# The state-space stage of a hybrid decoder step: 46 projection blocks as three rounded products each, with the rests subtracted on VectorE, the first convolution tap on ScalarE, and the group norm at a later place

## The chip, the cores and the metric

The program runs on one core of one Trainium2 chip. The metric is the device time of one execution in microseconds (us). The core has TensorE (PE: matrix products; its weight loads are PEld), VectorE (DVE), ScalarE (ACT), GpSimd (POOL) and SyncE (SP, which here only issues transfers). Each engine takes its own instructions strictly in order and waits on semaphores for the others.

## The reference, cut to what matters

One inference step of a decoder layer for 512 prompt tokens and 8 x 4 sample tokens (544 columns in all), with three branches (latent attention, state space, memory attention), a gated merge and a feed-forward part. Before the branches stands one projection of the 1024-wide input. The change lies in the state-space branch:

```
xbc = silu(conv_b + sum(conv_w[k] * xbc_ext[:, k:k + L] for k in range(4)))     # 24 chunks of 128 channels
per chunk of 128 tokens:
    y = (C.B * decay * dt) @ x + C @ S * exp(cum);   S = S * exp(last) + (wb * B).T @ x
y = (y + d_skip * x) * silu(z)
yg = y per group of 512 channels (4 groups);  yg *= rsqrt(mean(yg * yg) + eps);  y = yg * ssm_norm_g
```

All numbers are float32, and the matrix products have to come out near that precision.

## The kernel before, in words

Everything is kept transposed: channels on the 128 partitions, the 544 tokens on columns. The weights come as a stream of blocks of 128 x 1024 floats (512 KB) into a ring of four slots (`RING`); one block gives 128 output channels over all 544 tokens, written as two halves of 272 columns to one of two PSUM accumulators, `acc0` and `acc1`, in turn. `project` (L1721, matmuls at L1731) multiplies a block: 2 halves x 8 chunks = 16 float32 matmuls. SyncE's `load` (L552) fetches a block when the block three before it has begun (`blocks_begun`).

The state-space stage is block 0 (dt, 32 channels, L1841), blocks 1 to 6 (the six convolution chunks of group 0) and ten blocks for each of the four groups. The later stages (`out`, `up`, `down`) already use the other way: ScalarE rounds a block to the format fp32r (L701), GpSimd subtracts the rounded part from the block (L522), and `products` (L1771) multiplies in three passes of fp32r: high x high, high x low, low x high, 48 matmuls a block.

In this text the ten blocks of a group g are called b1 to b10. b1 to b4 are the four z chunks of group g; b5 to b10 are the convolution chunks 0 to 5 of group g+1 (in the last group: five latent chunks and the rotary one). Between them TensorE does the group's own products: it turns x and B (`turn`, before and inside b2, after b2), multiplies B by C (inside b3), adds up chunk states (before b4), reads out the four head pairs (`read_out` 0 to 3: before b5, before b6, before b8, before b9), and does the sample states (`sample_y` before b7, `state_adds` inside b7, before b8, inside b8, inside b9).

ScalarE empties an accumulator for a convolution chunk (`evac`, L715 to L718), or reads a z chunk (`z_read`, L775, L776), computes the decays (`decays`, L789 to L793) and the tanh of the gates (L724). VectorE does the convolution (`conv`, L1198: the left edge L1200, two small saves L1202 and L1203, the first tap L1208, three more taps L1214), closes the gate (`finish`, L1222 and L1224), weighs the decays (L1316), reads out y (L1369), gates it (L1374), adds the sample states (`add_state`, L1379), and norms the group before: a reciprocal (`group_reciprocal`, L1271) and four products (`group_norm`, L1276). GpSimd scales C (L470) and the sample states (L476) and adds squares (L482 to L488). The order of each engine's queue is written out by hand in these functions; nothing reorders it.

## Time and profile before

| | us |
|---|---|
| median of 3 executions | 1715.8 (1713.83 to 1717.81) |
| the profiled execution | 1717.8 |
| its span in the profile | 1716.1 |
| PE busy | 1667.9 (97%) |
| DVE busy | 758.8 (44%) |
| ACT busy | 408.4 (24%) |
| POOL busy | 405.9 (24%) |

Busy is the sum of an engine's instructions, over the whole span. The engines' shares differ much from stage to stage: the stage of this change takes the first 456 us. Times in the trace are counted from the start of the span. A matmul in float32 is recorded as two instructions (x32 is one block of 16), one in fp32r as one; the duration of the whole run of them is what counts.

### The profile page before, as it was taken

The page shows a single profiled execution, that of the slowest core. Times are in us where ns is not written, and L with a number is a line of the kernel's source. Part 1 is how long each engine was busy: PE and PEld are TensorE (multiplying, and loading weights), DVE is VectorE, ACT ScalarE, POOL GpSimd, SP SyncE. Part 2 cuts the span into 40 slices and gives each one's busy share as a digit, 9 for nine tenths or more (in the row PEclk, how much of TensorE's full clock was granted, in tenths as well). Part 3 has the DMA queues.
Part 4 walks back from the last instruction along what each step waited for, and adds up shares of the span by engine and source line. Part 5 has one row for each costly group of instructions (what it writes and reads, how often), then busy time and mean ns, then how long its engine had stood idle before and what let it go on. Part 6 is the DMA issues. An engine that isn't in the chain of part 4 may idle for free.

```text
span 1716.1 us, 25873 instructions
## 1 busy us (share of the span) xinstructions
PE 1667.9 (97%) x10438; PEld 1410.6 (82%) x10438; DVE 758.8 (44%) x1312; ACT 408.4 (24%) x800; POOL 405.9 (24%) x344
## 2 busy tenths in 40 slices
PE   8999999999999999999999999999996999999995
PEld 6878787787877777787777777779996999999995
DVE  5567687774431111112122122344378761177334
ACT  2252433425221211111111110142234111111122
POOL 0041231314020000000332300014345333344432
PEclk9999999999999999999999999999998999999998
DMA  5425133352362221223787764432321322222211
GB/s 193 148 80 175 66 124 123 94 179 80 114 212 71 62 74 62 62 77 117 229 254 235 236 241 181 151 123 87 99 86 39 89 93 89 86 87 87 87 62 53
DMA packets 70411, 206.24 MB, mean 120 GB/s; under 512 B 10162, under 2 KB 26803, under 8 KB 65683
## 3 DMA queue, kind: packets, MB, share of 16 engines
q1 hardware_dynamic: 50384, 151.67, 27.5%
q10 hardware_dynamic: 13762, 31.93, 5.3%
q0 software_dynamic: 6144, 20.98, 4.0%
q8 instruction: 83, 1.36, 0.3%
q14 instruction: 38, 0.30, 0.1%
HBM read 189.68 MB, written 14.86 MB: 119 GB/s over the span
## 4 chain that ended last, share of the span: by engine, by line
PE 87%; DVE 8%; issue 1%; ACT 1%; DMA 1%; POOLq 0%; POOL 0%; SPq 0%; DVEq 0%; ACTq 0%
PE acc L1731 29%; PE acc L1771 29%; PE acc L2069 7%; PE acc L2036 3%; PE acc L2019 2%; PE acc L2172 1%; PE bank L2084 1%; PE bank L2103 1%; PE bank L2085 1%; PE bank L2124 1%; DVE work L1214 1%; PE bank L2186 1%; PE bank L2054 1%; PE bank L2060 1%; PE bank L2257 1%
## 5 line engine op out<-in xcount | busy, mean ns | idle before, releaser
L1731 PE MATMUL acc<-xt,ring 128*128 128x272 f32 x2272 | 542.7, 395 | 0.0
L1731 PEld LDWEIGHTS acc<-xt,ring 128*128 128x128 f32 x2272 | 425.9, 190 | 99.5 <-issue 15.7
L1771 PE MATMUL acc<-x_parts,f_parts 128*128 128x272 f32 x1408 | 220.5, 293 | 12.4 <-DVE x_parts L1141 11.4
L522 POOL TENSOR_TENSOR f_parts<-ring,f_parts 128x1024 fp32r<-128x1024 f32 x65 | 157.6, 2425 | 247.9 <-ACT f_parts L701 247.7
L1771 PEld LDWEIGHTS acc<-x_parts,f_parts 128*128 128x128 f32 x1408 | 197.6, 192 | 14.4 <-issue 8.0
L500 POOL DMA_DIRECT2D work<-in_page_cols x128 | 68.8, 538 | 464.2 <-PE bank L2124 354.3
L1771 PE MATMUL acc<-f_parts 128*128 128x272 f32 x1344 | 172.3, 289 | 0.0
L1771 PEld LDWEIGHTS acc<-f_parts 128*128 128x128 f32 x1344 | 170.4, 188 | 0.1
L701 ACT ACTIVATE f_parts<-ring 128x1024 fp32r<-128x1024 f32 x65 | 69.0, 1061 | 238.4 <-PE acc L1771 204.2
L2069 PE MATMUL acc<-branch,ring 128*128 128x272 f32 x512 | 120.0, 392 | 0.0
L2069 PEld LDWEIGHTS acc<-branch,ring 128*128 128x128 f32 x512 | 96.0, 190 | 18.8
L1694 DVE TENSOR_SCALAR f_parts<-attended 128x544 fp32r<-128x544 f32 x32 | 76.2, 2382 | 1.1
L1214 DVE SCALAR_TENSOR_TENSOR work<-work,vecs 128x600 f32<-128x600 f32 x72 | 68.4, 950 | 2.4
L1771 PE MATMUL acc<-f_parts,mg_parts 128*128 128x272 f32 x528 | 68.8, 289 | 0.0
L1771 PEld LDWEIGHTS acc<-f_parts,mg_parts 128*128 128x128 f32 x528 | 67.3, 188 | 0.2
L522 POOL TENSOR_TENSOR mg_parts<-ring,mg_parts 128x1024 fp32r<-128x1024 f32 x21 | 50.5, 2403 | 71.4 <-ACT mg_parts L701 71.4
L1731 PE MATMUL acc<-attended,ring 128*128 128x272 f32 x256 | 63.1, 406 | 0.5 <-DVE attended L1603 0.5
L1771 PE MATMUL acc<-x_parts,mg_parts 128*128 128x272 f32 x480 | 62.1, 289 | 0.5 <-DVE attended L1688 0.5
L1771 PEld LDWEIGHTS acc<-x_parts,mg_parts 128*128 128x128 f32 x480 | 61.0, 188 | 0.7 <-DVE attended L1688 0.7
L1731 PEld LDWEIGHTS acc<-attended,ring 128*128 128x128 f32 x256 | 50.0, 197 | 12.3 <-issue 1.2
L1678 DVE TENSOR_TENSOR xt<-xt,acc 128x544 f32<-128x544 f32 x11 | 7.9, 721 | 111.8 <-PE acc L1771 111.8
L470 POOL TENSOR_TENSOR work<-work 128x384 f32<-128x384 f32 x32 | 37.1, 1158 | 75.2 <-ACT work L793 75.2
(351 smaller groups left out, 2046.3 us busy)
## 6 DMA issues: line engine op xcount, KB each, us to landing
ring<-in_stream SPq DMA_DIRECT2D x216, 512.0 KB, 3.6
work<-in_page_cols POOLq DMA_DIRECT2D x128, 160.0 KB, 3.3
attended<-in_ssm_state ACTq DMA_DIRECT2D x8, 1024.0 KB, 6.3
work<-cum_rows SPq DMA_DIRECT2D x32, 256.0 KB, 4.5
out_ssm_s<-attended ACTq DMA_DIRECT2D x8, 1024.0 KB, 5.5
work<-in_ckv_rows ACTq DMA_DIRECT2D x64, 128.0 KB, 3.5
work<-in_ckv_rows SPq DMA_DIRECT2D x64, 128.0 KB, 3.1
work<-in_memk_cols SPq DMA_DIRECT2D x8, 1024.0 KB, 6.7
```

The lines of the kernel that those rows point to most:

```text
L470: pool.tensor_tensor(r, r, C_[:, P:SEQ], MUL).then_inc(sem["c_scaled"], 1)
L500: pool.dma_start(keys[kq][:, i * KEYS_W:(i + 1) * KEYS_W], page_cols[p]).then_inc(sem[f"keys_in_slot{kq}"], 16)
L522: pool.tensor_tensor(lo, ring[:, s * BLOCK:(s + 1) * BLOCK], hi.bitcast(F), SUB).then_inc(sem["split_ready"], 1)
L701: act.activation(hi, ring[:, s * BLOCK:(s + 1) * BLOCK], ACT.Copy).then_inc(sem["hi_ready"], 1)
L1214: dve.scalar_tensor_tensor(out=c, in0=ext[j][:, i:i + CL], scalar=tap(i), in1=c, op0=MUL, op1=ADD).then_inc(sem[signal], 1)
L1694: dve.tensor_scalar(hi, q, 1.0, None, MUL).then_inc(sem["dve_step"], 1)
L1731: m = pe.matmul(acc[p][:, half, 0:width], w[:, k * P:(k + 1) * P], x(kk)[:, half * width:(half + 1) * width], start=kk == 0, stop=kk == n_ ...
L1771: m = pe.matmul(acc_half, w[:, k * P:(k + 1) * P], x[:, kk, of], start=kk == 0 and n == 0, stop=kk == last and n == 2)
L2019: m = pe.matmul(acc[p][:, 0, 0:N_MEM], w[:, k * P:(k + 1) * P], mem[:, k, :], start=k == 0, stop=k == KC - 1)
L2036: m = pe.matmul(acc[p][:, half, 0:HT], w[:, c * 256 + off:c * 256 + off + P], cq[:, c, half * HT:(half + 1) * HT], start=c == 0, stop=c == 2)
L2054: m = pe.matmul(bank[0][:, :], w[:, c * P:(c + 1) * P], ckv[:, c, 0:SEQ], start=c == 0, stop=c == 1)
L2069: m = pe.matmul(acc[1][:, half, 0:HT], w[:, k * P:(k + 1) * P], BR[:, kk, half * HT:(half + 1) * HT], start=kk == 0, stop=kk == 2 * KC - 1)
```

## The change

For blocks 1 to 46 (`SSM_SPLIT`) `project` gives way to `project_x` with three fp32r products, as in the later stages. The input x is split once at the start: ScalarE rounds its 8 chunks into XL, VectorE turns XL into the rest, and ScalarE then writes the rounded part over x itself (`xt_hi` lies where `xt` lay), chunk by chunk as the dt block has read it. Each weight block is rounded by ScalarE into one of two buffers (`high_part`), and VectorE writes the rest back over the ring slot (`low_part`). The rounding of a block waits until the block before it has begun. x is loaded again at the first block after the stage, and the memory tokens are loaded at the end of the stage instead of early. ScalarE now does the left edge and the first tap of each convolution chunk, right behind its evacuation, and VectorE starts a chunk on `tap_ready`. The halving of some constants goes to the start of VectorE's queue. The reciprocal and the four products of the group norm go from the first part of a group to between b6 and b9.

```
+            def high_part():                              # ScalarE
+                at = hi_at.next()
+                if at > SSM_SPLIT:
+                    return
+                s = at % RING
+                act.wait_ge(sem["blocks_begun"], CREDIT["blocks_begun"] + at)
+                act.wait_ge(sem[f"weights_in_slot{s}"], 16 * (loaded_before(at, s) + 1))
+                act.activation(w_hi[at % 2], ring[:, s * BLOCK:(s + 1) * BLOCK], ACT.Copy).then_inc(sem["hi_ready"], 1)
...
             def evac(j):
+                high_part()
+                n = evacuated.next()
+                ch = n - 1
+                if n > 2:
+                    act.wait_ge(sem["conv_ready"], n - 2)
+                act.activation(ext_s(j)[:, :, 0:3], st_conv[:, ch, :, :], ACT.Copy)
                 act.wait_ge(sem[f"acc{j}_ready"], t.next(f"acc{j}_ready"))
                 act.activation(v2(ext[j][:, 3:3 + T]), accv(j), ACT.Copy)
...
+                act.wait_ge(sem[f"acc{j}_free"], t.next(f"acc{j}_free"))
+                act.activation(cacc[j][:, 0:CL], ext[j][:, 0:CL], ACT.Identity, scale=tap,
+                        bias=V("convb", ch)).then_inc(sem["tap_ready"], 1)
...
                 def z_read(hp):
                     j, a = hp % 2, (hp + 1) % 2
+                    high_part()
...
+            def low_part():                               # VectorE
+                at = lo_at.next()
+                if at > SSM_SPLIT:
+                    return
+                slot = slice(at % RING * BLOCK, (at % RING + 1) * BLOCK)
+                dve.wait_ge(sem["hi_ready"], t.next("hi_ready"))
+                dve.tensor_tensor(ring_lo[:, slot], ring[:, slot], w_hi[at % 2].bitcast(F),
+                        SUB).then_inc(sem["split_ready"], 1)
...
             def conv(g, q, between=None):
                 j, ch = (q + 1) % 2, g * QC + q
-                dve.tensor_scalar(ext_s(j)[:, :, 0:3], st_conv[:, ch, :, :], 1.0, None, MUL)
-                dve.wait_ge(sem[f"acc{j}_free"], t.next(f"acc{j}_free"))
+                low_part()
+                dve.wait_ge(sem["tap_ready"], t.next("tap_ready"))
...
-                dve.tensor_scalar(c, ext[j][:, 0:CL], tap(0), V("convb", ch), MUL, ADD).then_inc(sem["dve_step"], 1)
...
+            low_part()
             conv(0, 0)
...
+                low_part()
                 z_gate(0)
                 turned(2, 3)
-                if g:
-                    group_reciprocal()
                 turned_samples()
-                if g:
-                    group_norm(g - 1)
+                low_part()
...
                 weigh(5)
+                if g:
+                    group_reciprocal()
                 read_y(1)
...
                 ahead_finish(1)
+                if g:
+                    group_norm(g - 1, (0, 1))
                 add_state(2)
...
+            def project_x(p, between=None):               # TensorE
+                at = used.value()
+                next_block()
+                wh, wl = w_hi[at % 2], ring_lo[:, at % RING * BLOCK:(at % RING + 1) * BLOCK]
+                pe.wait_ge(sem[f"acc{p}_free"], t.next(f"acc{p}_free"))
+                pe.wait_ge(sem["split_ready"], t.next("split_ready"))
+                for half, of in enumerate(halves):
+                    if half and between:
+                        between()
+                    for k in range(KC):
+                        if at == 1 and half == 0:
+                            pe.wait_ge(sem["x_split"], t.next("x_split"))
+                        first, m = products(acc[p][:, half, 0:HT], wh, wl, XH, XL, k, k, KC - 1, of)
...
+            sp.wait_ge(sem["y_ready"], GC * GROUPS)
+            sp.dma_start(mem, mem_t).then_inc(sem["mem_loaded"], 16)
+            load(3)
+            sp.wait_ge(sem["blocks_begun"], CREDIT["blocks_begun"] + SSM_SPLIT + 2)
+            sp.dma_start(X, x_t).then_inc(sem["x0_loaded"], 16)
```

`low_part` is called ten times in a group: for b3 ahead of `z_gate(0)`, for b4 behind the turned samples, for b5 in the middle of the state sums, for b6 ahead of `z_gate(3)`, and then at the head of each of the six `conv`, for b7 to b10 and the next group's b1 and b2. ScalarE's `high_part` for a block stands at the head of the evacuation of the block two before it.

The first place is the head of VectorE's queue, from its first instruction on. Before, it holds the dt computation alone (32 rows) and then the convolution:

```order
L1148 TENSOR_SCALAR work<-acc,vecs 32x544
L1152 SCALAR_TENSOR_TENSOR work<-work 32x544
L1156 TENSOR_SCALAR work<-work 32x544
L1158 TENSOR_SCALAR work<-work 32x544
L1161 TENSOR_SCALAR work<-work 32x544
```

Now (L1126 is the rest of x, L1121 the rest of a weight block):

```order
L1126 TENSOR_TENSOR ssm_parts<-xt,ssm_parts 128x544 x8
L1121 TENSOR_TENSOR ring_lo<-ring,ssm_parts 128x1024
L1135 TENSOR_SCALAR vecs<-vecs 128x24
L1135 TENSOR_SCALAR vecs<-vecs 128x120
L1138 MEMSET work 128x3 x2
L1248 TENSOR_SCALAR work<-acc,vecs 32x544
```

The rest of block 1 is made ahead of the dt computation, that of block 2 behind all of it.

The second place is VectorE's queue in groups 1 and 2 around b8, from the first two sample states to the third and fourth. Before (L1379 the sample states, L1200 to L1214 one convolution chunk, L1222 and L1224 the gate of the one before):

```order
L1379 TENSOR_TENSOR attended<-attended,bank 128x512 x2
L1200 TENSOR_SCALAR work<-work 128x8x3
L1202 TENSOR_SCALAR work<-work 128x3
L1203 TENSOR_SCALAR work<-work 128x24
L1208 TENSOR_SCALAR work<-work,vecs 128x600
L1214 SCALAR_TENSOR_TENSOR work<-work,vecs 128x600 x3
L1222 SCALAR_TENSOR_TENSOR branch<-work 128x512
L1224 SCALAR_TENSOR_TENSOR branch<-work 128x32
L1379 TENSOR_TENSOR attended<-attended,bank 128x512 x2
```

Now (the sample states are L1469, the chunk L1293 to L1302, the gate L1310 and L1312, two products of the group norm L1365):

```order
L1469 TENSOR_TENSOR attended<-attended,bank 128x512 x2
L1121 TENSOR_TENSOR ring_lo<-ring,ssm_parts 128x1024
L1293 TENSOR_SCALAR work<-work 128x3
L1294 TENSOR_SCALAR work<-work 128x24
L1302 SCALAR_TENSOR_TENSOR work<-work,vecs 128x600 x3
L1310 SCALAR_TENSOR_TENSOR branch<-work 128x512
L1312 SCALAR_TENSOR_TENSOR branch<-work 128x32
L1365 SCALAR_TENSOR_TENSOR branch<-branch,vecs,work 128x544 x2
L1469 TENSOR_TENSOR attended<-attended,bank 128x512 x2
```

Between the two pairs of sample states a rest (L1121) and two norm products have come in; the left edge and the first tap have gone.

The third place is ScalarE's queue at the end of the same group, for the chunks of b7 and b8. Before (L717 and L718 empty an accumulator, L724 is a gate's tanh, L833 a square):

```order
L833 ACTIVATE work<-branch 128x544 x2
L717 ACTIVATE work<-acc 128x544
L718 ACTIVATE work<-acc 128x8x4
L724 ACTIVATE work<-work 128x600
L717 ACTIVATE work<-acc 128x544
L718 ACTIVATE work<-acc 128x8x4
```

Now (L710 is the rounding of the block after the next, L784 the left edge, L791 the first tap):

```order
L710 ACTIVATE ssm_parts<-ring 128x1024
L784 ACTIVATE work<-work 128x8x3
L786 ACTIVATE work<-acc 128x544
L787 ACTIVATE work<-acc 128x8x4
L791 ACTIVATE work<-work,vecs 128x600
L796 ACTIVATE work<-work 128x600
```

The evacuation now stands behind a rounding, which itself waits for the next block to begin.

## Rows read from the trace of the kernel before

**Rows 1.** Engines by stretch, one row per group: length, busy (instructions), PEclk, DMA share, GB/s
```profile
core 0: us, PE busy (x) PEld busy (x) DVE busy (x) ACT busy (x) POOL busy (x), PEclk, DMA share, GB/s
70.94:169.38 98.44, 97.80 (x553) 76.43 (x553) 67.45 (x115) 34.53 (x82) 25.66 (x21) 1.00 0.35 115
169.38:268.66 99.28, 97.89 (x553) 76.42 (x553) 73.57 (x120) 38.00 (x85) 25.62 (x21) 1.00 0.36 120
...
367.93:456.38 88.45, 87.25 (x499) 68.44 (x500) 42.87 (x62) 35.98 (x76) 24.04 (x20) 1.00 0.30 100
```

**Rows 2.** Chain that ended last: start, length, what (one float32 block; four product blocks)
```profile
192.76 7.33 PE acc L1731 x32
...
1252.54 24.14 PE acc L1771 x192
```

**Rows 3.** Timeline of group 1, starts of b7 and b8, and two decays on ScalarE
```profile
192.80 1.28 ACT L789 ACTIVATE work<-work 128x128 f32<-128x128 f32 x4 [2.88 <-PE bank L1925]
...
195.06 1.26 ACT L789 ACTIVATE work<-work 128x128 f32<-128x128 f32 x4
...
222.60 3.93 PE L1731 MATMUL acc<-xt,ring 128*128 128x272 f32 x16
...
232.85 3.83 PE L1731 MATMUL acc<-xt,ring 128*128 128x272 f32 x16
```

**Rows 4.** Chain that ended last, start of b9 in group 1
```profile
243.12 3.86 PE acc L1731 x16
```

**Rows 5.** Timeline of the first phase: dt on VectorE, blocks 1 to 3 on TensorE
```profile
14.82 22.27 PE L1731 MATMUL acc<-xt,ring 128*128 128x272 f32 x96
15.03 0.77 DVE L1148 TENSOR_SCALAR work<-acc,vecs 32x544 f32<-32x544 f32 x1 [15.03 <-PE acc L1841]
...
30.14 0.22 DVE L1185 COPY work<-work 32x128 f32<-32x128 f32 x1
```

**Rows 6.** VectorE by form, 138.48 to 237.77: busy, mean ns | idle before
```profile
L1208 DVE TENSOR_SCALAR work<-work,vecs 128x600 f32<-128x600 f32 x6 | 4.1, 688 | 0.2
...
L1271 DVE RECIPROCAL work<-work 128x544 f32<-128x544 f32 x1 | 3.5, 3541 | 0.0
L1276 DVE SCALAR_TENSOR_TENSOR branch<-branch,vecs,work 128x544 f32<-128x544 f32 x4 | 2.9, 781 | 0.0
...
L1288 DVE TENSOR_TENSOR work<-bank,work 128x512 f32<-128x512 f32 x4 | 2.7, 683 | 2.4 <-PE bank L1896 2.4
```

**Rows 7.** VectorE by form, 1100 to 1716: a subtraction of a rounded part
```profile
L1640 DVE TENSOR_TENSOR f_parts<-xt,f_parts 128x544 fp32r<-128x544 f32 x8 | 5.2, 717 | 0.3 <-ACT f_parts L985 0.3
```

**Rows 8.** ScalarE, the rounding of a block (costliest groups of the page)
```profile
L701 ACT ACTIVATE f_parts<-ring 128x1024 fp32r<-128x1024 f32 x65 | 69.0, 1061 | 238.4 <-PE acc L1771 204.2
```

**Rows 9.** ScalarE by form, 138.48 to 237.77: gate and evacuation
```profile
L724 ACT ACTIVATE work<-work 128x600 f32<-128x600 f32 x6 | 4.2, 701 | 17.9 <-DVE work L1214 17.9
...
L717 ACT ACTIVATE work<-acc 128x544 f32<-128x544 f32 x6 | 3.7, 621 | 17.2 <-PE acc L1731 17.2
```

**Rows 10.** Timeline of group 1: three taps with and without GpSimd beside them
```profile
197.48 1.10 POOL L470 TENSOR_TENSOR work<-work 128x384 f32<-128x384 f32 x1 [0.76 <-ACT work L793]
...
213.07 3.23 DVE L1214 SCALAR_TENSOR_TENSOR work<-work,vecs 128x600 f32<-128x600 f32 x3
...
214.43 1.23 POOL L470 TENSOR_TENSOR work<-work 128x384 f32<-128x384 f32 x1 [2.76 <-ACT work L793]
...
232.46 2.60 DVE L1214 SCALAR_TENSOR_TENSOR work<-work,vecs 128x600 f32<-128x600 f32 x3
```

**Rows 11.** Timeline: a longer pause of TensorE (in brackets)
```profile
990.79 1.08 PE L2120 MATMUL bank<-work 128*32 128x256 f32 x16 [2.06 <-DMA work<-in_page_cols]
```

**Rows 12.** Timeline: a shorter one
```profile
1019.50 3.73 PE L2186 MATMUL bank<-work,branch 128*128 128x256 f32 x16 [1.09 <-DVE mark L1598]
```

**Rows 13.** Stretches behind the two pauses (PEclk third from the end)
```profile
992.00:993.00 1.00, 1.00 (x9) 0.32 (x5) 0.00 (x0) 0.00 (x0) 0.00 (x0) 0.54 0.79 271
...
995.00:996.00 1.00, 1.00 (x7) 0.86 (x5) 0.68 (x2) 0.00 (x0) 0.00 (x0) 0.75 0.21 66
...
1021.00:1022.00 1.00, 1.00 (x7) 0.86 (x6) 0.37 (x2) 0.00 (x0) 0.00 (x0) 1.00 1.06 434
```

**Rows 14.** The stretch in which the memory keys are computed
```profile
463.00:470.00 7.00, 7.00 (x34) 6.11 (x33) 6.96 (x7) 1.26 (x3) 0.00 (x0) 1.00 0.50 150
```

More of the change, by code:

```diff
@@ L163 @@
               "o_m_ready", "mg_ready"]
-SEMAPHORES += [f"{n}_in_slot{i}" for n in ("keys", "rows") for i in range(4)]
+SEMAPHORES += [f"{n}_in_slot{i}" for n in ("keys",) for i in range(4)]
 SEMAPHORES += [f"x{c}_loaded" for c in range(KC // 2)]
@@ L263, in program @@
         k = Carver()
-        ext, cacc, th = ([k(EXT) for _ in range(2)] for _ in range(3))
+        XH, XL = chunks(xt_hi, KC), chunks(ssm_parts, KC)
+        w_hi = [ssm_parts[:, KC * T + j * BLOCK:KC * T + (j + 1) * BLOCK] for j in range(2)]
+        ext, cacc = ([k(EXT) for _ in range(2)] for _ in range(2))
+        th = [work[:, j * EXT + 3:(j + 1) * EXT + 3] for j in range(2)]
+        st_conv = k(NC * DEC_BATCH * 3).rearrange("p (c b t) -> p c b t", b=DEC_BATCH, t=3)
+        assert B_S_AT <= k.at
+        b_s = rounded_b[0:NS3, k.at - B_S_AT:k.at - B_S_AT + P]
+        k.at += P
+        dec_p = k(NB * SSM_HEADS).rearrange("p (c h) -> p c h", h=SSM_HEADS)
+        k.at = 6 * T
+        off_s = k(GW)
+        c_mask = k(DEC_BATCH * NS).rearrange("p (b t) -> p b t", t=NS)
+        ecum_s = k(SSM_HEADS)
+        k.at = 6 * EXT
         krope, a_rstd = k(T), k(T)
@@ L294, in program @@
         xw = k((NB + 1) * GW).rearrange("p (c n) -> p c n", n=GW)
-        xdt_at = k.at
+        xw_s = rounded[0:NS3, xw_at - ROUNDED_AT + NB * GW:xw_at - ROUNDED_AT + (NB + 1) * GW]
         xdt = k((NB + 1) * GW).rearrange("p (c n) -> p c n", n=GW)
-        xw_s = rounded[0:NS3, xw_at - ROUNDED_AT + NB * GW:xw_at - ROUNDED_AT + (NB + 1) * GW]
         xw_full = xdt[NS:2 * NS, NB, :]
-        mem = k(KC * N_MEM).rearrange("p (c m) -> p c m", m=N_MEM)
+        assert k.at <= parts_at
+        k.at = WORK - GC * SEQ
+        cum_r = [k(SEQ) for _ in range(4)]
+        mem_at = WORK - KC * N_MEM
+        mem = work[:, mem_at:WORK].rearrange("p (c m) -> p c m", m=N_MEM)
+        mv_at = 22282
+        mk_at = mv_at + 2 * 1024
+        assert mk_at + 8 * N_MEM <= mem_at
         decay = [xw[:, c, :] for c in range(NB)]
@@ L460, in _ @@
                 pool.wait_ge(sem["cb_read"], t.next("cb_read"))
+                pool.wait_ge(sem["add_ready"], t.next("add_ready", NB))
                 if g:
@@ L1036, in _ @@
             t = Counts(dve, {"acc0_free": 1, "acc1_free": 1})
+            lo_at = Count(None)
+            def low_part():
[6 more added lines that the diff above has]
+                        SUB).then_inc(sem["split_ready"], 1)
+            for c in range(KC):
+                dve.wait_ge(sem["rounded"], t.next("rounded"))
+                dve.tensor_tensor(XL[:, c, :], X[:, c, :], XL[:, c, :].bitcast(F), SUB).then_inc(sem["low_even"], 1)
+            t.skip("low_even", KC)
+            low_part()
             dve.wait_ge(sem["const_loaded"], 2 * 16)
@@ L1039, in _ @@
             dve.wait_ge(sem["acc0_free"], 1)
+            w0 = _V["convw"][0]
+            g0 = _V["bgate"][0]
+            for halved in (vecs[:, g0:g0 + 3 * KC], vecs[:, w0:w0 + NC * (CONV_W + 1)]):
+                dve.tensor_scalar(halved, halved, 0.5, None, MUL).then_inc(sem["dve_step"], 1)
+            dve.wait_ge(sem["dve_step"], t.next("dve_step", 2))
+            for j in range(2):
+                dve.memset(ext[j][:, 0:3], 0.0).then_inc(sem["dve_step"], 1)
+            dve.wait_ge(sem["dve_step"], t.next("dve_step", 2))
             def maxima(pairs, scale, signal):
@@ L1272, in group_reciprocal, with group_norm @@
                 dve.wait_ge(sem["dve_step"], t.next("dve_step"))
-            def group_norm(g):
-                for hp in range(GC):
+            def group_norm(g, hps=range(GC)):
+                for hp in hps:
                     dve.scalar_tensor_tensor(out=BR[:, g * GC + hp, :], in0=BR[:, g * GC + hp, :],
@@ L2151, in cached_values @@
                     pe.wait_ge(sem["s_new_turned"], t.next("s_new_turned"))
-                    for kq in range(4):
-                        pe.wait_ge(sem[f"rows_in_slot{kq}"], t.next(f"rows_in_slot{kq}", 4 * 16))
+                    pe.wait_ge(sem["rows_loaded"], t.next("rows_loaded", 16 * 16))
                     for i in range(4):
```

152 lines of the change are left out of this document (91 added, 61 removed).

## The prediction

> **What bounds the kernel now.** I first read the engines by stretch, cut at the starts of b2 [rows 1]. In groups 0 to 2 TensorE is busy for 97.8 of about 99 us and VectorE for 67 to 74; the last group takes 88.45. So TensorE's work sets the time, and VectorE is second with some 26 us to spare a group. The chain that ended last says the same [rows 2]: one float32 block runs 7.33 us from first to last matmul, unbroken. It also has the price of the new way: four product blocks take 24.14 us, 6.04 each. Ten blocks a group are 73 of TensorE's 99 us, the other 26 are the group's own products.
>
> Next to read is how tight the queues beside TensorE are, since the change puts ten roundings into ScalarE's queue, ten rests into VectorE's, and each product block must wait for both. For that I take single durations from the groups by form [rows 6 to 9] and lay one group out, engine by engine, in queue order.
>
> **Prices.** A product block saves 7.33 - 6.04 = 1.29 us of TensorE; 46 blocks, 59 us. A rounding is 1.06 us [rows 8]. A rest is not in the trace at this size: the same subtraction with 544 columns takes 0.72 [rows 7], 512 columns of another take 0.68 [rows 6], so 1.06 ns a column and 1.23 us for 1024, 1.15 when the next follows at once. I take 1.2; the ends are 0.95 (a float32 tensor-scalar form of the first tap, 0.69 for 600 columns [rows 6], scaled by columns, 1.17 at most) and 1.8 beside GpSimd (below). The first tap costs VectorE 0.6 to 0.7 today and the left edge 0.2; on ScalarE the tap is like its gate, 0.70 for the same 600 columns [rows 9]. So VectorE gains 10 x 1.2 and loses 6 x 0.8: 73.6 becomes 81 us a group, under TensorE's 86. By sums alone a group would be 86.5 us. It is the order that spoils it.
>
> **The start.** The dt block ends at 14.8 and VectorE then works on dt until 30.36; TensorE meanwhile runs blocks 1 to 3 without a gap, until 37.1 [rows 5]. Splitting x hides under the loads and the dt block (8 roundings and 8 rests of 0.7 us, done at about 12; the last rounded chunk 0.7 us after the dt block, and TensorE begins with the first). But the rest of block 2 stands behind the whole dt computation. Block 1 ends at 21, block 2 can begin at 30.4 + 1.2 = 31.6: TensorE idles 10.6 us. Then each block waits for the rest made behind the convolution of the chunk three before it. Counting through I get starts of blocks 2 to 7 at 31.6, 37.7, 45.1, 52.1, 58.2, 64.2, the sixth chunk done at 71.4, and b2 of group 0 at 73.2 instead of 70.9: 2.3 us lost.
>
> **One group (1 or 2), from the start of b2 as zero.** Starts before, from [rows 2 to 4], less 169.38, and after, as laid out:
>
> b4: 23.4, now 19.5. b7: 53.2, now 47.6. b8: 63.5, now 60.5. b9: 73.7, now 74.6. Next b2: 99.3, now 99.3.
>
> To b7 the group runs 5.6 us ahead: five faster blocks bring 6.4, reciprocal and norm (3.5 and 2.9 [rows 6]) are out of VectorE's way in b3, and about 2.3 go lost before b5. There the decays wait behind the rounding for b5, which waits for b4 to begin at 19.5: rounding, z3 and the sample decays until 22.1, two decays of 2.26 (start to start [rows 3]), and 1.1 for GpSimd's product [rows 10], so the read-out starts at 27.9 and not at 25.6.
>
> Then it is lost again, in three places.
> - *Inside b7.* `state_adds(0)` needs `read_y_s`, and VectorE gets to that so: weights 4 and 5 until 46.6, the reciprocal until 50.1, read-out 0.7, rest 1.2, one tap 0.9, `read_y_s` 0.7: 53.7. b7's first half is done at 50.6. TensorE waits 3.1.
> - *Inside b8.* VectorE ends sample states 0 and 1 at 60.1, and b8 can begin at 60.5. Only then does ScalarE round for b9 (61.65), and only behind that evacuate b7 (0.7) and do the tap (0.7): `tap_ready` at 63.15, though b7 was finished at 57.3. VectorE stands idle for 2 us, then saves, three taps 2.8, gate 0.83, two norm products 1.43, two sample states 1.2: 69.5. b8's first half is done at 63.5, TensorE waits 6 us. Before, the same stretch of VectorE's queue went on without a wait.
> - *At the end.* b9 begins at 74.6, so b10's rounding is ready at 75.8 and VectorE idled 3.6 us; the last chunk is gated at 97.4, while TensorE is through with b1 and the sums at 94.1: a wait of 3.3.
>
> These waits cost 12 us or so of the 12.8 that ten blocks save. The whole is even: 99.3.
>
> Two costs come on top. *GpSimd.* Three taps took 2.60 us alone and 3.23 with a GpSimd operation of 1.23 among them [rows 10]: half of the shared time is lost. On VectorE's tight stretch from 46 to 97 some 11 us of GpSimd work lie; about a quarter of it hits VectorE where it is late: 1.5 a group (0.5 in the last). *The clock.* After a pause of 2.06 us TensorE was granted 0.54, the 1.2 GHz level, from 992 on, though busy, and half of the slice from 995 still (0.75); after a pause of 1.09 it stayed at 1.00 [rows 11 to 13]. That is some 3.3 us at half speed, so I price a pause like this or longer at 3.3 / 2 = 1.65 beside itself, where TensorE is on the path behind it. That is so for two of the pauses in each of groups 0 to 2 (in b8, and at the end; the one in b7 has a spare us behind it), for one in group 3, and for the one at the start. Bounds: 0, and 3 for each.
>
> **Group 0** has no reciprocal and no norm: 95.8 laid out instead of 98.44. **Group 3** has no convolution ahead, so TensorE leads from b5 on: 81.2 instead of 88.45.
>
> **Behind the stage** x comes again, 2.2 MB, ahead of the block for the fourth memory key. The stretch moves 150 GB/s [rows 14] and 434 have been seen [rows 13], so both land 7 to 9 us after the issue, and the block is wanted 10.4 us (three of 3.47) after it: nothing, at most 2. The memory tokens come 1 MB, some 12 us before they are used: nothing.
>
> **Sum.** Start +2.3 and 1.65; group 0 -2.6 + 1.5 + 3.3; groups 1 and 2 twice 0 + 1.5 + 3.3; group 3 -7.2 + 0.5 + 1.65. Together +10.7. Against the profiled execution, 1717.8, that is 1728.5; this execution was 2.0 above the median of 1715.8, so I expect 1726.5. Its own range, with 2 us either way a group and the bounds of the clock: 1716 to 1742.
>
> **A rule against the trace.** The trace shows half of the shared time lost [rows 10]. The Trainium skill (SBUF — State Buffer, Who interferes with whom) says that a VectorE instruction with two SBUF inputs and a GpSimd instruction that reads SBUF exclude each other, and the second waits for the whole first. The rest is such an instruction and there are ten new ones a group; it would make the collisions dearer, the third rival below.
>
> **Rivals.**
> - *The waits are there, but they cost only themselves* (no clock loss, no collisions on the tight stretch). For: the shorter pause left the clock alone, and ten of GpSimd's operations fall in VectorE's own waits. Against: the pauses laid out are 3 to 6 us. Time: 1715.8 + 2.3 - 2.6 + 0 - 7.2 = 1708. It is the case on the other side; it decides as soon as the two extra costs stay under 7.5 us in all.
> - *TensorE stays the bound.* If ScalarE and VectorE keep up everywhere, 59 us less the 10.6 of the start: 1667. Against it: the evacuation of b7 and b8 cannot precede the next block's start, whatever the speeds.
> - *Collisions whole.* If each of the nine GpSimd operations on the tight stretch costs VectorE its whole 1.1 us and not a fraction, a group loses 10 and not 1.5: three times 8 more, 1750.
> - *In between:* half of the extra costs of 18.2 us, 1717.
>
> **How the numbers follow.** Forecast 0.53, waits alone 0.22, TensorE bound 0.05, whole collisions 0.08, in between 0.12. Below 0.2% (3.4 us) a measurement of this kernel can't be told from no change. Faster takes the second and third case and a little of the last: 0.29; same most of the last and the low edge of the forecast: 0.10; slower 0.61. The range that leaves out the bound case and the far ends of the others is 1702 to 1744.
>
> **What would show it.** TensorE idle from about 21 to 31.6, and b2 of group 0 at 73 to 76. Starts of b2 99 to 106 us apart in groups 1 and 2. In b7, b8 and at the group's end, TensorE waiting for VectorE, the longest (5 to 6 us) for the sample states in b8, and PEclk near 0.5 behind them. Rests of 1.2 us, up to 1.8 beside GpSimd. VectorE waiting for the first tap and for roundings. Wrong it is if b8 begins long before VectorE's first two sample states are in, if the evacuations come right behind their blocks, or if the groups shrink under 97 us.

## The result, and the profile after

The changed kernel takes 1754.4 us (median of 4 runs, 1751.51 to 1756.54) against 1716.7 for the kernel before on the same chip: ratio 1.0221, interval 1.0205 to 1.0238. Slower was forecast, at 1726.5; the measured time lies 10 us above the end of the range, 1744. The profiled execution is the one of 1751.51 us, span 1749.8, against 1717.8 and 1716.1 before: 33.7 us to explain.

The page of the changed kernel, its busy line, TensorE's granted clock in 40 slices, and the chain by engine:

```profile
PE 1635.0 (93%) x11174; PEld 1434.6 (82%) x11174; DVE 794.9 (45%) x1318; ACT 483.5 (28%) x910; POOL 404.1 (23%) x344
...
PEclk8998989989999999999999999999998999999998
...
PE 81%; DVE 9%; ACT 5%; issue 3%; DMA 1%; POOL 0%; POOLq 0%; ACTq 0%; SPq 0%; DVEq 0%
```

The first eleven slices of the clock are the changed stage. The stretches that answer to [rows 1], cut at the same places (groups 0 to 3 and the memory keys); columns as there:

```profile
76.97:184.55 107.58, 91.88 (x713) 83.02 (x713) 74.22 (x115) 49.76 (x104) 25.16 (x21) 0.92 0.31 101
184.55:293.93 109.38, 91.15 (x713) 82.24 (x713) 79.12 (x118) 53.21 (x107) 25.17 (x21) 0.92 0.34 109
293.93:406.43 112.50, 93.19 (x714) 84.07 (x713) 79.83 (x118) 53.21 (x107) 24.71 (x21) 0.91 0.33 109
406.43:492.95 86.52, 79.38 (x644) 71.91 (x644) 50.29 (x68) 44.50 (x86) 23.27 (x20) 0.96 0.34 113
492.95:528.15 35.20, 34.51 (x159) 29.41 (x158) 20.20 (x21) 5.64 (x13) 4.47 (x8) 1.00 0.67 226
```

TensorE was busy for 97.8 of 98 to 99 us of each group; now it is busy for 91 to 93 and stands for 16 to 19. The groups grew by 9.1, 10.1 and 13.2 us, the last one shrank by 1.9, and b2 of group 0 comes at 77.0 instead of 70.9, 6.0 later. The sum is 36.6; the memory keys take 0.5 more than before, and the code behind them, which the change leaves alone, 3.3 less in this execution (its granted clock is 0.99 there and was 0.98). What TensorE waited for, from 15 to 500 us (total, times, longest):

```profile
PE bank L2099 <- DVE attended L1469: 17.0, 4, 5.6
PE bank L2099 <- DVE branch L1488: 16.2, 4, 4.7
PE bank L2014 <- DVE work L1312: 14.5, 4, 4.7
PE acc L1869 <- DVE ring_lo L1121: 10.4, 3, 10.0
PE bank L2058 <- POOL work L500: 7.9, 3, 2.7
PE bank L2058 <- DVE work L1405: 3.7, 1, 3.7
```

In this order: inside b8, inside b7, at the group's end, before block 2, before the read-out ahead of b5 in groups 0, 1 and 3, the same in group 2. All places are those laid out; the sizes are not.

### The profile page after: what moved, and what is told of

Its sections match the earlier page's. It is cut to its first block, busy times and chain, and to the rows that moved or that the text cites. A ratio compares the mean times of both kernels' runs of the same rounds, so it can differ in the third digit from the quotient of the medians.

```text
span 1749.8 us, 27506 instructions
## 1 busy us (share of the span) xinstructions
PE 1635.0 (93%) x11174; PEld 1434.6 (82%) x11174; DVE 794.9 (45%) x1318; ACT 483.5 (28%) x910; POOL 404.1 (23%) x344
## 4 chain that ended last, share of the span: by engine, by line
PE 81%; DVE 9%; ACT 5%; issue 3%; DMA 1%; POOL 0%; POOLq 0%; ACTq 0%; SPq 0%; DVEq 0%
PE acc L1869 38%; PE acc L1829 14%; PE acc L2188 7%; PE acc L2155 3%; DVE work L1302 2%; PE acc L2290 1%; ACT work L864 1%; ACT ssm_parts L710 1%; PE acc L2137 1%; PE bank L2058 1%; PE bank L2203 1%; PE bank L2222 1%; PE bank L2204 1%; PE bank L2243 1%; PE bank L2304 1%
## 5 line engine op out<-in xcount | busy, mean ns | idle before, releaser
L1869 PE MATMUL acc<-xt_hi,ssm_parts 128*128 128x272 f32 x736 | 226.7, 308 | 10.4 <-DVE ring_lo L1121 10.4
L1869 PE MATMUL acc<-x_parts,f_parts 128*128 128x272 f32 x1408 | 221.0, 293 | 11.9 <-DVE x_parts L1241 10.7
L1869 PE MATMUL acc<-ssm_parts 128*128 128x272 f32 x736 | 219.5, 298 | 0.0
L1869 PE MATMUL acc<-xt_hi,ring_lo 128*128 128x272 f32 x736 | 219.3, 298 | 0.0
L1829 PE MATMUL acc<-xt,ring 128*128 128x272 f32 x800 | 191.9, 396 | 0.0
L1829 PEld LDWEIGHTS acc<-xt,ring 128*128 128x128 f32 x800 | 149.4, 190 | 35.1 <-issue 6.0
L1869 PEld LDWEIGHTS acc<-xt_hi,ssm_parts 128*128 128x128 f32 x736 | 147.1, 200 | 21.7 <-issue 20.6
L1869 PEld LDWEIGHTS acc<-ssm_parts 128*128 128x128 f32 x736 | 147.3, 200 | 2.0 <-issue 1.0
L1869 PEld LDWEIGHTS acc<-xt_hi,ring_lo 128*128 128x128 f32 x736 | 146.0, 198 | 0.0
L1121 DVE TENSOR_TENSOR ring_lo<-ring,ssm_parts 128x1024 fp32r<-128x1024 f32 x46 | 63.5, 1379 | 94.2 <-ACT ssm_parts L710 94.0
L710 ACT ACTIVATE ssm_parts<-ring 128x1024 fp32r<-128x1024 f32 x46 | 48.7, 1059 | 184.4 <-PE acc L1869 172.5
```

The lines of the kernel that those rows point to most:

```text
L710: act.activation(w_hi[at % 2], ring[:, s * BLOCK:(s + 1) * BLOCK], ACT.Copy).then_inc(sem["hi_ready"], 1)
L1121: dve.tensor_tensor(ring_lo[:, slot], ring[:, slot], w_hi[at % 2].bitcast(F), SUB).then_inc(sem["split_ready"], 1)
L1829: m = pe.matmul(acc[p][:, half, 0:width], w[:, k * P:(k + 1) * P], x(kk)[:, half * width:(half + 1) * width], start=kk == 0, stop=kk == n_ ...
L1869: m = pe.matmul(acc_half, w[:, k * P:(k + 1) * P], x[:, kk, of], start=kk == 0 and n == 0, stop=kk == last and n == 2)
```

## The experiments

Twelve kernels ran, each timed against the kernel before (1713.8 to 1715.5 in these comparisons, 1716.7 beside the changed kernel). "Less" and "more than the changed kernel" are differences of medians; with the kernel before beside each as the measure, every one comes out 1 to 3 us less favourable to the altered kernel. Starts of b2 and of the memory keys' first product give the lengths of groups below, the last "group" then being 92.9 us for the changed kernel and 94.8 before.

### Keeping TensorE busy in its pauses

```diff
+ def keep_busy(out, n):
+     for i in range(n):
+         pe.matmul(out, XH[:, i % KC, 0:P], XH[:, i % KC, 0:HT], start=True, stop=True)
  # project_x, ahead of between(), in b7 and b8: 24 products into the half that is overwritten next
+                     if half and fill:
+                         keep_busy(acc[p][:, 1, 0:HT], fill)
  # group's end, ahead of the wait for conv_ready, groups 1 to 3
+                     keep_busy(bank[0][:, 0:HT], 20)
```

> The changed kernel with idle products added (they compute nothing that is read) in three places of each group where TensorE pauses: 24 products of 272 columns (some 3 us) ahead of the state adds inside block 7, 24 ahead of those inside block 8, 20 ahead of the wait for the last convolution chunk at the group's end (groups 1 to 3). TensorE gets about 25 us more to do. Theory 'clock': what lengthened the groups beyond the laid-out waits is the half-rate stretch behind each pause (about 1.7 to 2 us more for the 24 products behind it, the granted clock 0.50 to 0.66 there), so with no long pause left the blocks behind run at 3.0 to 3.2 us a half, the granted clock of groups 1 and 2 rises from 0.92 to 0.97 or more, and the kernel, though it does more, is 10 to 18 us faster than the changed kernel: 1736 to 1744 us. Rival 'waits and collisions only': the pauses are set by VectorE and nothing behind them depends on the clock; the time stays within 1750 to 1758, or rises where a fill outlasts its pause (1 us each, to 1765).

1740.1 us (ratio 1.0145, 1.0127 to 1.0164), 14.3 less than the changed kernel, with 252 more products on TensorE: the clock theory's range, not the rival's. First the changed kernel behind the three long pauses of group 1, in b7, in b8 and at the group's end, in slices of 3 us (the granted clock is third from the end), then the filled one, groups 0 to 2:

```profile
240.00:243.00 3.00, 1.93 (x7) 1.77 (x8) 2.89 (x8) 0.50 (x2) 0.86 (x1) 0.50 0.00 0
243.00:246.00 3.00, 3.00 (x15) 3.00 (x15) 2.97 (x7) 1.61 (x3) 0.43 (x1) 0.51 0.02 5
...
258.00:261.00 3.00, 3.00 (x11) 2.60 (x12) 2.97 (x5) 0.00 (x0) 0.00 (x0) 0.50 0.00 0
261.00:264.00 3.00, 3.00 (x18) 2.85 (x18) 0.14 (x1) 0.00 (x0) 0.00 (x0) 0.66 0.00 0
...
290.00:293.00 3.00, 2.42 (x12) 2.42 (x12) 2.58 (x7) 0.00 (x0) 0.73 (x1) 0.56 0.00 0
293.00:296.00 3.00, 3.00 (x25) 2.34 (x25) 1.83 (x4) 1.71 (x3) 0.00 (x0) 0.88 0.28 49
```

```profile
76.41:179.68 103.27, 95.45 (x784) 86.86 (x781) 73.37 (x113) 49.78 (x104) 25.21 (x21) 0.98 0.32 106
179.68:285.27 105.59, 95.60 (x783) 86.88 (x780) 79.13 (x118) 53.23 (x107) 25.19 (x21) 0.98 0.34 113
285.27:390.73 105.46, 94.24 (x784) 85.56 (x781) 80.16 (x118) 53.25 (x107) 24.74 (x21) 1.00 0.35 117
```

The pauses themselves are not shorter: in group 2 TensorE stood 19.3 us before; now 11.2 and 68 fill products, which at the 0.126 us of full speed are 8.5. What went is the half rate. Group 2 at a clock of 1.00 has 94.2 - 8.5 = 85.7 us of own work; the changed kernel was busy for 91.15 and 93.19 with the same work, so the clock cost it 5.4 and 7.5 us in groups 1 and 2. From the slices, the pause in b7 costs (1 - 0.50) x 1.93 + (1 - 0.51) x 3.00 = 2.4 us, the one in b8 (1 - 0.50) x 3.00 + (1 - 0.66) x 3.00 = 2.5, and the one at the end (1 - 0.56) x 2.42 + (1 - 0.88) x 3.00 = 1.4. That is 6.4 where the busy time gives 5.4: the slices count every busy us behind a pause as if half of it were lost, so I take them as an upper figure. The prediction had 1.65, for two pauses a group.

Group 2 is dearer because there the pause before b5, 3.74 us long, is a fourth one that costs the clock. In groups 0 and 1 this pause has the same length, 2.66 and 2.65 us, and not the same price. The slices behind it in the changed kernel, group 1 and then group 0, and last those behind a pause of 1.50 us in b8 of group 3:

```profile
213.00:216.00 3.00, 2.83 (x37) 2.69 (x38) 0.30 (x1) 0.71 (x1) 0.02 (x1) 1.00 0.02 5
105.00:108.00 3.00, 2.42 (x27) 2.45 (x28) 0.71 (x1) 0.00 (x0) 0.44 (x1) 0.67 0.00 0
108.00:111.00 3.00, 3.00 (x22) 2.67 (x20) 0.87 (x1) 1.96 (x3) 0.00 (x0) 0.76 0.29 60
...
472.00:475.00 3.00, 2.02 (x11) 1.66 (x12) 2.97 (x6) 0.00 (x0) 0.00 (x0) 0.94 0.00 0
475.00:478.00 3.00, 3.00 (x15) 3.00 (x15) 1.04 (x2) 0.00 (x0) 0.00 (x0) 0.50 0.00 0
```

So a pause near 2.6 us may cost nothing or (1 - 0.67) x 2.42 + (1 - 0.76) x 3.00 = 1.5, and one of 1.50 us cost (1 - 0.94) x 2.02 + (1 - 0.50) x 3.00 = 1.6: length alone does not tell. Those of 3.7 us and more all cost. Read in slices of half a microsecond, fourteen pauses of the stage cost the clock: one at the start, four in group 0, three in group 1, four in group 2, two in group 3. Eight of them cost 1.6 to 1.7 us each, five (those in b7 of groups 0 to 2 and in b8 of groups 1 and 2) 2.4 to 2.8, the one at the start 3.0; 29.4 in all.

The Trainium skill (TensorE: Matmul & The Clock Gate, HAM oscillation — how this bites in real kernels) describes this form of loss: waits that return in a loop make TensorE pay the change of clock again each time. By that rule the clock would be lost in every group, and the trace agrees: 0.91 or 0.92 in each of groups 0 to 2 and 0.96 in group 3.

### ScalarE empties first

```diff
  def evac(j):
-     high_part()
      ...                                   # emptying, first tap
+     high_part()
  def conv(g, q, between=None):
-     low_part()
      dve.wait_ge(sem["tap_ready"], t.next("tap_ready"))
      ...                                   # three taps
+     low_part()
```

> The changed kernel with the order on two engines turned round for the 24 convolution blocks: ScalarE empties the accumulator and does the first tap before it rounds the next weights (1.06 us), and VectorE subtracts the rest after its three taps instead of before the wait for the first tap. Theory 'coupling': each chunk is finished some 1 to 2 us earlier behind its block, so the pause at the group's end (3.9 to 4.7 us) and the one before block 8 shrink by 1 to 2 us each, and their clock price may go with them: 6 to 20 us faster than the changed kernel, 1734 to 1748. Rival 'rests become late': the rest of the next block now stands behind three taps (about 3 us), TensorE waits for it at the block's start instead; then waits on the rests show in TensorE's row and the time is 1750 to 1775.

1727.1 us (ratio 1.0063, 1.0044 to 1.0081): 27.3 us less than the changed kernel, by order alone, more than my theory's upper end of 20. The timelines of ScalarE in group 1, at the emptying of b7's accumulator (L786, in the altered kernel L785), say why. b7 ends at 246.97 in the changed kernel and at about 239.98 in this one. The first fence shows what TensorE does between b7 and b8 in the changed kernel (rows of its chain), the second ScalarE there (L710 is the rounding), the third ScalarE in the altered kernel:

```profile
246.97 0.59 PE bank L2058 x8
...
248.66 0.67 PE bank L2099 x2
249.33 0.14 PE acc L1869
```

```profile
249.49 1.06 ACT L710 ACTIVATE ssm_parts<-ring 128x1024 fp32r<-128x1024 f32 x1 [4.00 <-PE acc L1869]
...
250.57 0.61 ACT L786 ACTIVATE work<-acc 128x544 f32<-128x544 f32 x1
```

```profile
239.98 0.62 ACT L785 ACTIVATE work<-acc 128x544 f32<-128x544 f32 x1 [0.78 <-PE acc L1869]
...
240.73 0.89 ACT L790 ACTIVATE work<-work,vecs 128x600 f32<-128x600 f32 x1
242.46 1.06 ACT L710 ACTIVATE ssm_parts<-ring 128x1024 fp32r<-128x1024 f32 x1 [0.84 <-PE acc L1869]
```

In the changed kernel the rounding in front waits for b8's first product, and b8 stands behind a read-out and two state adds: 2.5 us. With the rounding's own 1.06 the emptying comes 3.6 us behind the block. Here it comes at once. TensorE's standing time in group 1 falls from 18.2 to 13.0 us (102.56 long, 89.60 busy), the clock rises from 0.92 to 0.95.

Which engine's order did it?

```diff
  def conv(g, q, between=None):            # VectorE alone; ScalarE as changed
-     low_part()
      ...
+     low_part()
```

> The changed kernel with one engine's order altered alone: VectorE subtracts the rest of the next weights after the three taps of a convolution chunk instead of before the wait for the first tap; ScalarE rounds first and empties afterwards, as changed. With both engines' orders turned round the kernel measured 1727.1, 27 us less than the changed one. Theory 'VectorE's order in front of the chunk': most of those 27 us come from here, since it is the rest (1.2 to 2.1 us, and its wait for the rounding) that stood in front of the taps: 1728 to 1738. Rival 'ScalarE's order': the rounding (1.06 us) ahead of the emptying delays both, and with it left there the gain is half or less: 1739 to 1752.

1760.7 us (1.0276, 1.0259 to 1.0293): 6 us slower than the changed kernel. My theory falls, and so does the size that the rival gave (1739 to 1752). This kernel and the emptying-first one differ in ScalarE's order alone: 1760.7 against 1727.1, so with the rests last, emptying first is worth 33.6 us. What it is worth with the rests left in front was not run. The rest in front costs little, since VectorE subtracts it (1.23 us, from 250.59 in group 1) while ScalarE empties and taps, and then still waits 0.42 us for the tap; put last, with the rounding still in front of the emptying, it makes TensorE wait for rests:

```profile
PE acc L1869 <- DVE ring_lo L1121: 24.9, 9, 9.3
PE bank L2099 <- DVE attended L1469: 20.4, 4, 6.8
PE bank L2099 <- DVE branch L1488: 15.8, 4, 4.5
```

### The start

```diff
  # VectorE, dt computation
      dve.wait_ge(sem["dt_v"], t.next("dt_v"))          # behind w["abs"]
+     low_part()
      ...                                               # to the product r * u
+     low_part()
- low_part()                                            # behind the dt computation
  conv(0, 0)                                            # and none in chunk 0
  # ScalarE: the rounding of block 3 ahead of the Ln
```

> The changed kernel with the rests of blocks 2 and 3 subtracted inside the dt computation, in places where VectorE waits for ScalarE anyway, instead of behind the whole of it; ScalarE rounds block 3 before the Ln. Theory: the 9.8 to 10.4 us that TensorE stands before block 2 shrink to 2 to 4 us and the half-rate stretch behind them (31.8 to 38) goes, while the dt computation ends 1 to 2.5 us later; what counts is whether its end or TensorE is late then. 3 to 8 us faster than the changed kernel: 1746 to 1751. Rival 'the dt computation is the path at the start': the rests lengthen it and the gain is eaten there, within 2 us of 1754.

1743.1 us (1.0164, 1.0147 to 1.0181): 11.3 less, more than expected. The changed kernel's chain at the start (start, length), then one row of this kernel's:

```profile
30.49 1.14 DVE ring_lo L1121
31.77 14.97 PE acc L1869 x96
...
55.43 12.43 PE acc L1869 x97
```

```profile
31.77:64.76 32.99, 31.24 (x261) 29.76 (x259) 29.61 (x59) 15.96 (x32) 0.73 (x1) 1.00 0.56 179
```

Two blocks behind the pause take 14.97 us where two later ones take 12.43: 2.5 us for the clock, 10 for the pause. In this kernel neither is there and b2 of group 0 comes at 64.8, 12.1 earlier than in the changed kernel and 6.1 earlier than before the change.

### GpSimd's part

```diff
- pool.tensor_tensor(r, r, C_[:, P:SEQ], MUL)           # scaled C, 8 a group
+ pool.tensor_tensor(r[:, 0:1], r[:, 0:1], C_[:, P:P + 1], MUL)
- pool.tensor_tensor(by_head(st_s[:, b, :]), by_head(st_s[:, b, :]), heads(dec_s, b, g, P), MUL)
+ pool.tensor_tensor(st_s[:, b, 0:1], st_s[:, b, 0:1], st_s[:, b, 0:1], MUL)
```

> The changed kernel with GpSimd's two large kinds of work cut to one column each (the scaling of C for each head and the decay of the sample states are left out; the signals stay). To be read against the same cut in the kernel before. Theory 'collisions are the lesser part': the rests come down from 1.38 us a piece to about 1.23 and the 3-column copies to 0.17, worth 1.5 to 3 us a group; the difference between the changed kernel and the one before, 37.6 us whole, stays above 24 us with GpSimd cut in both. Rival 'collisions carry it': the difference falls under 15 us.

> The kernel before with the same two kinds of GpSimd's work cut to one column each (scaling of C and decay of the sample states left out). TensorE is busy nearly throughout there, so every theory expects little: 1708 to 1717 us.

Both kernels leave out the scaling of C and the decay of the sample states. 1742.5 us for the changed kernel so cut (11.9 less), 1714.8 for the one before (ratio 0.9998, no change). The difference falls from 37.6 to 27.7 us, so collisions with these two kinds of work and their lateness together are about 10 us of the 38. That is the lesser part, as expected, but twice the 5 us priced. The rests and the first small copies (VectorE, 15 to 500 us), changed kernel and then the cut one:

```profile
L1121 DVE TENSOR_TENSOR ring_lo<-ring,ssm_parts 128x1024 fp32r<-128x1024 f32 x45 | 62.2, 1383 | 94.2 <-ACT ssm_parts L710 94.0
L1293 DVE TENSOR_SCALAR work<-work 128x3 f32<-128x3 f32 x24 | 9.2, 385 | 6.7 <-ACT work L791 6.7
```

```profile
L1121 DVE TENSOR_TENSOR ring_lo<-ring,ssm_parts 128x1024 fp32r<-128x1024 f32 x45 | 59.8, 1329 | 95.4 <-ACT ssm_parts L710 95.2
L1293 DVE TENSOR_SCALAR work<-work 128x3 f32<-128x3 f32 x24 | 7.5, 313 | 7.4 <-ACT work L791 7.4
```

The rests did not come down to 1.23, against my expectation. GpSimd's other products and its shortened ones may still meet them; this was not separated.

### The norm, and the first tap

```diff
  # norm slots: in VectorE's queue
+ group_reciprocal()                # ahead of the state copies
+ group_norm(g - 1, (0, 1))         # ahead of the rest in front of z gate 3
+ group_norm(g - 1, (2, 3))         # behind the scaled sample part
- ...                               # behind weights 4 and 5, behind chunks 2 and 3
```

> The changed kernel with the group norm of the group before placed in VectorE's idle slots: the reciprocal (3.5 us) ahead of the state copies, where VectorE waits for TensorE, two of the norm's products ahead of the rest that stands before z gate 3, two behind the scaling of the sample part; they go from behind the weights 4, 5 and from blocks 8 and 9. Theory 'VectorE's order sets the pauses in blocks 7 and 8': the pause before the state adds of block 7 loses up to 3.5 us, that of block 8 some 1.5 to 3, in three groups: 8 to 16 us faster than the changed kernel, 1738 to 1746. Rival: the reciprocal then delays the state copies and the read-out instead (the pause before block 5 grows from 2.7 us by 2 to 3): 1750 to 1758.

1748.9 us, with runs from 1741.9 to 1752.5 (1.0208, 1.0191 to 1.0225, which overlaps the changed kernel's interval): 3 to 5 us by the medians, not clear of zero, and not 8 to 16. The pause inside b7 is as long as ever, with the reciprocal gone from in front of it:

```profile
PE bank L2098 <- DVE branch L1491: 15.6, 4, 4.8
```

What holds `read_y_s` there is ScalarE, whose queue has no gap from 225.12 on in this kernel: decays 4 and 5, a gate, decay 6, and only then the rounding that VectorE's next rest wants. ScalarE (rounding) and VectorE (rest) there:

```profile
235.06 1.04 ACT L710 ACTIVATE ssm_parts<-ring 128x1024 fp32r<-128x1024 f32 x1
```

```profile
236.14 1.70 DVE L1121 TENSOR_TENSOR ring_lo<-ring,ssm_parts 128x1024 fp32r<-128x1024 f32 x1 [1.64 <-ACT ssm_parts L710]
```

The rest waited 1.64 us with nothing else to do. In the changed kernel the reciprocal and that rounding end together, at 236.2, so taking one of them away leaves the other. Only the read-out behind the reciprocal (0.75 us) counted beside them: the rest begins 0.8 us earlier here, and the copy and the tap behind it lose that again beside GpSimd (1.00 and 1.45 us instead of 0.82 and 0.83).

```diff
  # norm back: as in the kernel before, around turned_samples() in b3
+ group_reciprocal()
  turned_samples()
+ group_norm(g - 1)
```

> The changed kernel with the group norm (reciprocal and four products, 6.6 us) back where the kernel before has it, around the samples' turned rows and ahead of the masked B C products: it prices the moved norm by itself. Theory: there it delays the state copies, the weights and so the read-out of TensorE ahead of block 5, by up to 6.6 us less the 1.9 us that VectorE waits there, in three groups, while blocks 7 and 8 win 3.5 and 1.5 to 3: within 6 us of the changed kernel, 1748 to 1760. Rival: the delay is passed on whole and pays a clock stretch, 1760 to 1772.

1751.0 us (1.0209, 1.0194 to 1.0225): 3 less than the changed kernel, intervals overlapping. Where the norm stands, of these three places, is worth nothing that can be told from zero.

```diff
- act.activation(cacc[j][:, 0:CL], ext[j][:, 0:CL], ACT.Identity, scale=tap, bias=V("convb", ch))
+ dve.tensor_scalar(c, ext[j][:, 0:CL], tap(0), V("convb", ch), MUL, ADD)
```

> The changed kernel with the first tap of each convolution chunk back on VectorE (0.76 us there against 0.90 on ScalarE), all else as changed: it prices this part of the change by itself. From the rows the chunk's chain is as long either way (0.90 + a signal against 0.76), but VectorE has 4.6 us a group more in its row, of which part stands in blocks 8 and 9 ahead of what TensorE waits for: 2 to 12 us slower than the changed kernel, 1756 to 1766. Rival: ScalarE was late with the roundings because of the taps, and the rests waited for it; then 2 to 8 us faster, 1746 to 1752.

1765.0 us (1.0301, 1.0285 to 1.0317), 10.6 slower, at the upper end of the expected 2 to 12: moving the first tap was the part of the change that helps.

### Putting the orders together

> The changed kernel with three orders altered together: emptying and first tap before the rounding and taps before the rest (24 convolution blocks), the rests of blocks 2 and 3 inside the dt computation, and the group norm in the idle slots. Nothing is left out and no product is added. The emptying-first order alone measured 1727.1, 27 us less than the changed kernel. If the pauses are independent, the start gives 3 to 8 and the norm 5 to 12 more: 1707 to 1719, so level with or under the kernel before (1715.5). Rival 'TensorE's waits move to the next producer' (the scaled C of GpSimd, the rounding): 1720 to 1727.

Emptying first, the start and the norm slots: 1716.8 us (1.0017, 1.0007 to 1.0026), 0.2% above the kernel before.

> The three orders altered together and the idle products of the filled pauses added (24, 24 and 20 products of 272 columns in blocks 7, 8 and at the group's end). Theory 'clock': the remaining pauses of 2 to 3.5 us still cost a half-rate stretch each, so filling them gives 3 to 10 us more: 1700 to 1712. Rival: with pauses this short the fills (2.5 to 3 us each) outlast them and delay the work behind, 3 to 10 us slower than without: 1714 to 1726.

1724.6 us (1.0056, 1.0039 to 1.0073), 7.7 slower than without the fills: the rival. The pauses in b7 and b8 without fills are 2.4 us at most there, and the fills take 2.5 to 3. A fill pays for a pause that stays; it is not a substitute for removing one.

The chain of the three orders runs through VectorE from b4 to b8, so one more step took work off it:

```diff
- dve.tensor_scalar(conv_out[:, ch, 0:3], ext[j][:, SEQ:EXT_P], 1.0, None, MUL)    # and the 24 columns
+ act.activation(conv_out[:, ch, 0:3], ext[j][:, SEQ:EXT_P], ACT.Copy)             # behind the first tap
```

> The three altered orders together (which measured 1716.8 against 1714.7 for the kernel before), and the two small copies of each convolution chunk's last columns (3 and 24 columns) moved from VectorE to ScalarE, behind its first tap. Theory 'VectorE's row is what bounds a group now': the chain of waits of the three orders runs through VectorE in blocks 5 to 8; the copies take 0.25 us alone and up to 1.2 beside GpSimd, in front of the taps, 24 times: 4 to 12 us faster than the three orders, 1705 to 1713, so under the kernel before. Rival: ScalarE's rounding, which now comes 0.3 us later per chunk, or another producer takes it up: 1713 to 1719.

1711.1 us (11 runs, 1710.06 to 1713.86) against 1714.7: ratio 0.9981, interval 0.9972 to 0.9990: faster by 0.2%, the size below which the prediction would not tell a difference from none. Groups 0 to 3, and TensorE's longest waits from 15 to 500 us:

```profile
69.73:166.14 96.41, 87.18 (x716) 78.45 (x713) 73.48 (x101) 51.83 (x116) 26.96 (x21) 0.98 0.35 113
166.14:266.29 100.15, 88.48 (x716) 79.47 (x713) 82.19 (x106) 55.20 (x119) 29.14 (x21) 0.97 0.36 119
266.29:367.07 100.78, 88.82 (x716) 79.85 (x713) 82.73 (x106) 55.18 (x119) 28.10 (x21) 0.97 0.37 122
367.07:458.35 91.28, 84.56 (x673) 75.52 (x671) 56.92 (x75) 46.35 (x89) 26.27 (x20) 0.98 0.33 113
```

```profile
PE bank L2103 <- DVE attended L1477: 8.4, 7, 2.4
PE bank L2062 <- POOL work L500: 7.9, 3, 2.7
PE bank L2018 <- DVE work L1318: 7.3, 4, 1.9
```

The pauses in b8, in b7 (4.6 us in all) and at the group's end are halved or less, those before b5 are as they were, and the clock is back to 0.97 or 0.98; yet TensorE still stands 11.7 us in group 1. VectorE is busy 82 of 100 us there and its row has to be met in order. Of the 59 us that TensorE's products save, 3.6 have reached the end.

## Why the prediction was wrong in size

Right were the direction, the places of the pauses and most starts: in group 1, from b2, b4 came at 19.9 (laid out 19.5) and b7 at 48.6 (47.6); then b8 at 64.8 (60.5), b9 at 81.2 (74.6) and the next b2 at 109.4 (99.3). The error grows pause by pause. By the prediction's terms:

- **Start: +2.3 + 1.65 predicted, +6.0 measured.** TensorE did stand until 31.77 (31.6). The clock took 2.5 (two blocks in 14.97 us for 12.43), not 1.65. The rest, 1.2, was not followed to its cause.
- **The clock, the step that failed.** "1.65 beside itself", for two pauses a group, 3.3. It measured 5.4 and 7.5 us in groups 1 and 2 (busy time beyond the 85.7 us of the filled kernel's own work). First the number of pauses was wrong: "the one in b7 has a spare us behind it" did not hold, b7's pause came out at 4.7 us and is paid for like the others, so there are three in group 1; with the one before b5 there are four in groups 0 and 2; two short ones cost it in group 3. The prediction priced eight pauses in the stage, and fourteen cost the clock. Second the price: 1.65 is what eight of the fourteen cost (1.6 to 1.7), but the pauses in b7 and b8 mostly cost 2.4 to 2.8, and the one at the start 2.5 to 3.0. So the 13.2 us priced were 25 (by busy time, group 3 by the slices) to 29 (all by the slices): at 1.65 each fourteen pauses make 23, so the count is the larger part. The bound of 3 each for two pauses, 6, does not hold group 2; for three it would.
- **The waits: 14.7 us a group laid out** (2.3 before b5, 3.1, 6 and 3.3), 18.2 and 19.3 measured in groups 1 and 2. In group 1: 2.6, 4.7, 5.6, 4.6. b8 was right; b7 and the end were 1.6 and 1.3 short. With "collisions 1.5" added, 2 to 3 us a group were missing. In b7 the cause named was half of it: the reciprocal is in the chain, but ScalarE's queue ends with it, and with the reciprocal gone the pause stays, as the norm slots showed.
- **Own work** 84.6 laid out (99.3 - 14.7), 85.7 by the filled kernel: 1.1. For group 1 that makes 1.1 + 5.4 + (18.2 - 14.7) = 10.0 over 99.3, measured 10.1; for group 2, 1.1 + 7.5 + 4.6 = 13.2, measured 13.2. These sums must close, since busy and standing time make up the length; how much of the busy part is clock and how much own work is sure to about 1 us only (by the slices own work is 84.6 and the clock 6.6 in group 1).
- **Group 0** -2.6 + 1.5 + 3.3 = +2.2 predicted, +9.1 measured, from the same terms (6.2 us of clock by busy time, 15.7 us of standing); **group 3** -7.2 + 0.5 + 1.65 predicted, -1.9 measured: pauses of 2.5, 1.5 and 2.6 us remain there, with the clock at 0.96; the first two cost it 1.7 us each.
- **Behind the stage** 0 predicted, 0.5 measured for the memory keys: right.
- **The taps and rests.** The first tap takes ScalarE 0.89 us, not 0.70, six times a group. A rest took 1.38 on average; 1.2 alone was right.
- **"The evacuation of b7 and b8 cannot precede the next block's start"** was given as a property of the change. It is only the order of two lines on ScalarE: turned round together with the rests it is worth 27 us. I had seen the wait and not priced what it costs over all 24 chunks.
- **The range.** "2 us either way a group and the bounds of the clock" make 1705 to 1745 when added up, not 1716 to 1742. The measured time lies beyond that too.

The rule of the Trainium skill (SBUF — State Buffer, Who interferes with whom) that spoke against the change, whole exclusion of VectorE and GpSimd, gave the rival of 1750, the nearest of the numbers, but not for its reason: with the larger part of GpSimd's work cut away 27.7 of 37.6 us remain. What stays open is how the clock's cost and the lengthening of the waits split between them in the 10 us of the GpSimd experiment; it removes lateness too, and a pause that shrinks also saves its clock.

## What to carry to other kernels

When work is taken off the engine that bounds a loop and put on its feeders, lay out the queues and then price each pause with its clock: here 1.6 to 2.8 us beside every pause of 3.7 us and more, even one that seemed to have slack, and 1.7 beside some of 1.5 to 2.7 us. In each feeder's queue, ask which instruction waits for the *next* step of the bound engine and what it holds up behind it; put the work that frees the current step first. If a pause must stay, independent products in it keep the clock (14 us here), but they should be shorter than the pause (7.7 us slower here where they were not).

## What the runs showed of the hardware

- Half rate after a pause: the two blocks behind the 10 us pause took 14.97 us for 12.43; a half block of 24 products behind pauses of 4.7 and 5.6 us took 4.7 for 3.0 to 3.2.
- Which pauses cost the clock does not follow from their length alone: 1.50, 2.51 and 2.66 us did in the changed kernel, 2.65 and 2.64 us did not.
- A copy of 3 columns on VectorE takes 0.17 us alone and 0.61 to 1.33 beside GpSimd, so a tiny instruction in front of a chain can cost as much as the subtraction of 1024 columns; three taps that follow each other lose only part of GpSimd's time (2.60 alone, 3.08 to 3.23 beside it).
- ScalarE's pass over 600 columns takes 0.89 us with a per-partition scale and bias and 0.70 as Tanh without them.
